# A one-core decoder layer kernel: its opening put in order of need, with small tables loaded later from the pool's queue

## What is computed

```
h = rmsnorm(x); h @ w_in -> [q_B | k_B | v_B | u_A | v_A | q_C | gate logits]
A: chunked gMLP gating, u * (W_s v + b), causal 128x128 W_s per group
B: dilated sliding-window attention with a relative bias; C: cross-attention into 256 memory rows
x = x + w_out( sig(g_A) P_A(A) + sig(g_B) P_B(B) + sig(g_C) P_C(C) )
x = x + MoE(rmsnorm(x))    top-4 of 32 experts;   y = rmsnorm(x)
memory keys and values: rmsnorm(mem_prompt) @ w_mem_kv
```

## Time and profile before

| | |
|---|---|
| median of 3 runs | 1539.71 us (1538.79 to 1542.64) |
| the profiled execution | 1539.54 us, span 1537.7 us |
| PE busy | 1409.7 us (92%) |
| ACT busy | 240.7 us (16%) |
| DVE busy | 374.8 us (24%) |
| POOL busy | 52.6 us (3%) |
| DMA | 515.17 MB, mean 335 GB/s |
| mean granted PE clock | 0.953 |

### The profile page before, as it was taken

One profiled execution on the slowest core, in us unless ns is written; L12 is line 12 of the kernel. 1 busy time (PEld: TensorE's weight loads), 2 busy tenths in 40 slices (PEclk: granted clock), 3 DMA queues, 4 the chain that ended last, 5 costly groups with the idle time before them and its releaser, 6 DMA issues.

```text
span 1537.7 us, 20357 instructions
## 1 busy us (share of the span) xinstructions
PE 1409.7 (92%) x8013; PEld 693.9 (45%) x8013; DVE 374.8 (24%) x858; ACT 240.7 (16%) x389; POOL 52.6 (3%) x90
## 2 busy tenths in 40 slices
PE   3999977997898779999999999999999999999995
PEld 1685535866786334343343433333343333333333
DVE  2100365420012152222222212222221222222123
ACT  2001011220001041121111111111121111112112
POOL 0100212002100000000000000000000000000000
PEclk9999877996599989999999999999999999999998
DMA  9535966239247657999999999999999999999994
GB/s 319 181 128 191 328 236 237 89 157 345 94 163 288 261 207 310 424 422 421 422 422 422 421 423 421 422 422 422 422 422 422 422 422 422 421 422 422 422 422 164
DMA packets 86697, 515.17 MB, mean 335 GB/s; under 512 B 10047, under 2 KB 11655, under 8 KB 36812
## 3 DMA queue, kind: packets, MB, share of 16 engines
q1 hardware_dynamic: 77504, 493.69, 79.3%
q0 software_dynamic: 6016, 18.83, 3.8%
q10 hardware_dynamic: 3148, 2.24, 0.5%
HBM read 511.21 MB, written 47.52 MB: 363 GB/s over the span
## 4 chain that ended last, share of the span: by engine, by line
PE 65%; DMA 21%; DVE 5%; SPq 4%; issue 2%; ACT 1%; ACTq 1%; POOL 0%; DVEq 0%
PE psum L524 62%; DMA weights<-in_w_gate_up 17%; SPq L424 4%; PE psum L527 3%; DMA weights<-in_w_out 2%; DMA weights<-in_cache_mem_kv 2%; DVE qk L1272 1%; ACTq L1325 1%; ACT qk L1328 0%; POOL weights L484 0%; DVE x L1297 0%; DVE kvt L1166 0%; DVE va L1179 0%; DVE hT L1242 0%; DVE kc L1177 0%
## 5 line engine op out<-in xcount | busy, mean ns | idle before, releaser
L524 PE MATMUL psum<-weights,wsp 128*64 128x512 f32 x2048 | 491.8, 603 | 15.2 <-DMA weights<-in_w_gate_up 14.4
L524 PE MATMUL psum<-weights,merged 128*64 128x512 f32 (+2 forms) x1152 | 274.3, 600 | 10.7 <-DMA weights<-in_w_out 9.2
L524 PEld LDWEIGHTS psum<-weights,wsp 128*64 128x64 f32 x2048 | 127.5, 136 | 266.8 <-issue 177.9
L1242 DVE TENSOR_TENSOR hT<-psum,hT 128x264 f32<-128x264 f32 x264 | 101.7, 427 | 529.4 <-PE psum L524 529.3
L524 PE MATMUL psum<-hT,weights 128*128 128x264 f32 x704 | 171.7, 403 | 13.8 <-DVE weights L984 9.1
L524 PEld LDWEIGHTS psum<-weights,merged 128*64 128x64 f32 (+2 forms) x1152 | 89.6, 141 | 167.0 <-issue 158.9
L524 PEld LDWEIGHTS psum<-hT,weights 128*128 128x128 f32 x704 | 138.2, 198 | 45.6 <-DVE weights L984 12.2
L524 PE MATMUL psum<-bT,merged 64*128 64x264 f32 x528 | 94.2, 434 | 1.1 <-ACT merged L1487 0.7
L1468 ACT COPY bT<-psum 128x264 f32<-128x264 f32 x33 | 12.5, 379 | 484.1 <-PE psum L527 484.0
L524 PEld LDWEIGHTS psum<-bT,merged 64*128 64x128 f32 x528 | 39.8, 184 | 106.7 <-issue 103.9
L1272 DVE TENSOR_SCALAR qk<-psum,lowest 128x512 f32<-128x512 f32 x64 | 48.0, 750 | 162.6 <-PE psum L524 159.2
(11 more groups left out here) (242 smaller groups left out, 765.3 us busy)
## 6 DMA issues: line engine op xcount, KB each, us to landing
weights<-in_w_gate_up SPq DMA_DIRECT2D x256, 1024.0 KB, 26.1
weights<-in_w_down SPq DMA_DIRECT2D x128, 1024.0 KB, 25.0
out<-in_cache_win_kv SPq DMA_DIRECT2D x8, 4094.0 KB
weights<-in_w_in SPq DMA_DIRECT2D x13, 2048.0 KB, 7.7
weights<-in_cache_mem_kv POOLq DMA_DIRECT2D x16, 512.0 KB, 7.8
out<-in_cache_win_kv SPq DMA_DIRECT2D x2, 4088.0 KB
weights<-in_cache_win_kv POOLq DMA_DIRECT2D x48, 128.0 KB, 6.1
weights<-in_w_mem_kv SPq DMA_DIRECT2D x2, 2048.0 KB, 14.4
```

Source lines behind the costliest of these rows:

```text
L524: return nc.tensor.matmul(out, lhsT, rhs, start=start, stop=stop, **kw)
L1242: V.tensor_tensor(acc[:, c, :], p_a[j % 2][part], acc[:, c, :], ALU.add).then_inc(s_acc, 1)
```

## The change

The list of steps begins with `vec` and `memT`; a step `xn` (root and scaling of x) stands between `memT` and `kc`; `rel`, `sbias` and `wsp` come between `q` and `k`. The memory rows arrive in two DMAs of 128 rows with a semaphore each. Ten table loads go from ACT's queue to POOL's, behind a wait for x. SP no longer waits for tables behind its first block. ACT runs one Sqrt on an unused column of `stat` before it waits for the memory rows.

```diff
--- before.py
+++ after.py
@@ -111,10 +111,9 @@
 
 def schedule():
 
-    s = [("vec",), ("wsp",)] + [("rel", g) for g in range(NG)] + [("sbias",)]
-    s += [("memT", k) for k in range(KD)] + [("kc", h) for h in range(CH)] + [("xT", k) for k in range(KD)]
+    s = [("vec",)] + [("memT", k) for k in range(KD)] + [("xn",)] + [("kc", h) for h in range(CH)] + [("xT", k) for k in range(KD)]
     s += [("vc", t) for t in range(2)] + [("kct", t) for t in range(2)]
-    s += [("q", m) for m in range(6)] + [("k", m) for m in range(6)]
+    s += [("q", m) for m in range(6)] + [("rel", g) for g in range(NG)] + [("sbias",), ("wsp",)] + [("k", m) for m in range(6)]
     s += [("v", t, 0) for t in range(3)] + [("v", t, 1) for t in range(3)]
     s += [("kt", t, n) for t in range(3) for n in range(2)] + [("qc", m) for m in range(4)]
     s += [("qs", 0), ("qs", 1), ("qcs",), ("vts",), ("selfb",)]
@@ -322,7 +321,8 @@
         s_sq, s_vecr, s_wsp, s_rel, s_sels, s_lnw, s_bsp, s_w00 = (sem("in_" + n) for n in (
             "square", "vectors", "wsp", "rel", "sample", "lnw", "bsp", "w00"))
         s_router_in, s_gfin_in, s_brow_in, s_grow_in = sem("in_router"), sem("in_gfin"), sem("in_brow"), sem("in_g_ffn_row")
-        s_mem_in, s_x_in, s_xagain = sem("in_mem"), sem("in_x"), sem("in_x_again")
+        s_mem_in = [sem(f"in_mem{t}") for t in range(2)]
+        s_x_in, s_xagain = sem("in_x"), sem("in_x_again")
         s_block_in = [sem(f"block_in{n}") for n in range(4)]
         s_chunk_in = [sem(f"chunk_in{n}") for n in range(CHUNKS)]
         s_used = sem("chunks_used")
@@ -363,7 +363,8 @@
         @block.sync
         def _(sp):
             with nc.allow_non_contiguous_dma(reason="small vectors"):
-                sp.dma_start(mem_tok, I["mem_prompt"][0].rearrange("(t p) c -> p t c", p=P)).then_inc(s_mem_in, 16)
+                for t in range(2):
+                    sp.dma_start(mem_tok[:, t, :], I["mem_prompt"][0, t * P:(t + 1) * P, :]).then_inc(s_mem_in[t], 16)
                 sp.dma_start(x1[:, 0:2, :], I["x_prompt"][0].rearrange("(t p) c -> p t c", p=P)).then_inc(s_x_in, 16)
                 sp.dma_start(x1[0:NS, 2, :], I["x_sample"][:, 0, :]).then_inc(s_x_in, 16)
             copies = []
@@ -384,11 +385,6 @@
                 if n >= 4:
                     sp.wait_ge(s_job, last_job[n - 4])
                 sp.dma_start(block_view(name, src.shape[0]), src).then_inc(s_block_in[n % 4], 16)
-                if n == 0:
-                    sp.wait_ge(s_vecr, 48)
-                    sp.wait_ge(s_wsp, 16)
-                    sp.wait_ge(s_rel, 32)
-                    sp.wait_ge(s_sels, 16)
                 if 10 <= n and copies:
                     shift(*copies.pop(0))
                 if name == "gc1":
@@ -467,6 +463,19 @@
         def _(pool):
             nc.gpsimd.iota(iota[:], [[1, SLOTS * PASSES]], base=1, channel_multiplier=0,
                            allow_small_or_imprecise_dtypes=True).then_inc(s_iota, 1)
+            pool.wait_ge(s_x_in, 32)
+            with nc.allow_non_contiguous_dma(reason="small vectors"):
+                pool.dma_start(wsp[:], I["w_spatial"][0].rearrange("g i j -> i g j")).then_inc(s_wsp, 16)
+                pool.dma_start(rel[0:REL_BUCKETS, :], I["rel_bias"]).then_inc(s_rel, 16)
+                pool.dma_start(selh.rearrange("p g x -> p (g x)"), C["hankel"]).then_inc(s_rel, 16)
+                pool.dma_start(sels.rearrange("p g x -> p (g x)"), C["sample"]).then_inc(s_sels, 16)
+                pool.dma_start(lnw[:, 0, :], I["ln_v_g"].to_broadcast([P, 512])).then_inc(s_lnw, 16)
+                pool.dma_start(lnw[:, 1, :], I["ln_v_b"].to_broadcast([P, 512])).then_inc(s_lnw, 16)
+                pool.dma_start(bsp[:].rearrange("p g i -> p (g i)"),
+                              I["b_spatial"].rearrange("d g i -> d (g i)").to_broadcast([P, AG * P])).then_inc(s_bsp, 16)
+                pool.dma_start(w00[:], I["w_spatial"][:, :, 0, 0].to_broadcast([P, AG])).then_inc(s_w00, 16)
+                pool.dma_start(wr[:], I["w_router"][0].rearrange("(k p) e -> p k e", p=P)).then_inc(s_router_in, 16)
+                pool.dma_start(br[:], I["b_router"].to_broadcast([P, E])).then_inc(s_router_in, 16)
             taken(pool, "rel", NG - 1)
             pool.dma_start(rel_rows[:].rearrange("g h x -> h g x"), hrow).then_inc(s_hstore, 16)
             pool.wait_ge(s_hstore, 16)
@@ -902,14 +911,6 @@
                 if t == 0:
                     seq(ins)
             ins.then_inc(s_done["memn"], 1)
-            rms_scale(stat[:, 2:5], D, 5)
-            dve.wait_ge(s_rt, 2)
-            seq(V.reciprocal(stat[:, 2:5], stat[:, 2:5]))
-            for t, (_, tn) in enumerate(TILES):
-                ins = V.tensor_scalar(x1[0:tn, t, :], x1[0:tn, t, :], stat[0:tn, 2 + t:3 + t], None, ALU.mult)
-                if t < 2:
-                    seq(ins)
-            ins.then_inc(s_done["xn"], 1)
 
             for s in steps:
                 kind, a = s[0], s[1:]
@@ -940,6 +941,15 @@
                     k, = a
                     ready()
                     V.tensor_scalar(memT[:, k, :], o[:, 0:NM], g_mem[:, k:k + 1], None, ALU.mult).then_inc(free, 1)
+                elif kind == "xn":
+                    rms_scale(stat[:, 2:5], D, 5)
+                    dve.wait_ge(s_rt, 2)
+                    seq(V.reciprocal(stat[:, 2:5], stat[:, 2:5]))
+                    for t, (_, tn) in enumerate(TILES):
+                        ins = V.tensor_scalar(x1[0:tn, t, :], x1[0:tn, t, :], stat[0:tn, 2 + t:3 + t], None, ALU.mult)
+                        if t < 2:
+                            seq(ins)
+                    ins.then_inc(s_done["xn"], 1)
                 elif kind == "xT":
                     k, = a
                     ready()
@@ -1312,25 +1322,15 @@
                 act.dma_start(sq[:], C["square"]).then_inc(s_sq, 16)
                 for n, name in enumerate(("norm_mix", "norm_mem", "norm_ffn")):
                     act.dma_start(vecr[n * KD:(n + 1) * KD, :], I[name][0].rearrange("(k p) -> k p", p=P)).then_inc(s_vecr, 16)
-                act.dma_start(wsp[:], I["w_spatial"][0].rearrange("g i j -> i g j")).then_inc(s_wsp, 16)
-                act.dma_start(rel[0:REL_BUCKETS, :], I["rel_bias"]).then_inc(s_rel, 16)
-                act.dma_start(selh.rearrange("p g x -> p (g x)"), C["hankel"]).then_inc(s_rel, 16)
-                act.dma_start(sels.rearrange("p g x -> p (g x)"), C["sample"]).then_inc(s_sels, 16)
-                act.dma_start(lnw[:, 0, :], I["ln_v_g"].to_broadcast([P, 512])).then_inc(s_lnw, 16)
-                act.dma_start(lnw[:, 1, :], I["ln_v_b"].to_broadcast([P, 512])).then_inc(s_lnw, 16)
-                act.dma_start(bsp[:].rearrange("p g i -> p (g i)"),
-                              I["b_spatial"].rearrange("d g i -> d (g i)").to_broadcast([P, AG * P])).then_inc(s_bsp, 16)
-                act.dma_start(w00[:], I["w_spatial"][:, :, 0, 0].to_broadcast([P, AG])).then_inc(s_w00, 16)
-                act.dma_start(wr[:], I["w_router"][0].rearrange("(k p) e -> p k e", p=P)).then_inc(s_router_in, 16)
-                act.dma_start(br[:], I["b_router"].to_broadcast([P, E])).then_inc(s_router_in, 16)
 
             def squares(dst, src, junk):
                 A.activation(junk, src, ACT.Square, accum_out=dst).then_inc(s_ss, 1)
 
             junk = merged[:, :, :].rearrange("p a b -> p (a b)")
             act.wait_ge(s_dve, 1)
-            act.wait_ge(s_mem_in, 16)
+            A.activation(stat[:, 39:40], stat[:, 39:40], ACT.Sqrt)
             for t in range(2):
+                act.wait_ge(s_mem_in[t], 16)
                 squares(stat[:, t:t + 1], mem_tok[:, t, :], junk[:, t * D:(t + 1) * D])
             act.wait_ge(s_ms, 1)
             A.activation(stat[:, 0:2], stat[:, 0:2], ACT.Sqrt).then_inc(s_rt, 1)
@@ -1338,8 +1338,6 @@
             junk2 = qk[:, :, :].rearrange("p a b -> p (a b)")
             for t, (_, tn) in enumerate(TILES):
                 squares(stat[0:tn, 2 + t:3 + t], x1[0:tn, t, :], junk2[0:tn, t * D:(t + 1) * D])
-            act.wait_ge(s_ms, 2)
-            A.activation(stat[:, 2:5], stat[:, 2:5], ACT.Sqrt).then_inc(s_rt, 1)
 
             for s in steps:
                 kind, a = s[0], s[1:]
@@ -1351,7 +1349,10 @@
                     def take(out, in_, name, n=n, free=free):
                         act.wait_ge(s_job, n + 1)
                         A.copy(out, in_).then_inc(free, 1)
-                if kind == "rel":
+                if kind == "xn":
+                    act.wait_ge(s_ms, 2)
+                    A.activation(stat[:, 2:5], stat[:, 2:5], ACT.Sqrt).then_inc(s_rt, 1)
+                elif kind == "rel":
                     take(hrow[:, a[0], :], o[0:HPG, 0:HANK], "hrow")
                 elif kind == "kc":
                     take(kcT[:, a[0], :], o[:, 0:NM], "kcT")

```

## The result

| | before | after |
|---|---|---|
| median, first runs | 1539.25 us, 4 runs (1538.56 to 1542.64) | 1524.22 us, 4 runs (1523.43 to 1524.48) |
| ratio | | 0.9895, 95% interval 0.9879 to 0.991 |
| the profiled execution | 1539.54 us, span 1537.7 | 1524.09 us, span 1522.3 |
| PE busy | 1409.7 us | 1407.8 us |
| POOL busy | 52.6 us | 59.5 us |

15.0 us less by the medians, 15.5 by the profiled executions and 16.2 by the ratio (13.9 to 18.6 by its interval), against 17.8 forecast: inside the range.

What follows compares the result with a forecast made beforehand. ACT's queue, issuing DMAs, was taken to bound the opening, PE everything from kc on. 21.5 gained less 3.7 lost gave 17.8 us: 1539.54 - 17.8 = 1521.7, given as 1521.8; range 1517.5 to 1527.5.

Steps and rivals of the forecast that it cites:

- The hinge: Start of kc in the opening: at 15.7 instead of 37.24 us, held by memk's landing, bringing all behind forward; 21.5 gained.
- the tables' share: In memk's landing: POOL's tables share the last 2 us of its transfer, adding 0.6 us.
- The fit of the Trainium skill: memk's transfer as 2.0 us plus bytes at 436 GB/s: landing at 13.1, memT then bounds; as a rival 1520.3, 17%.
- ACT's chain: In the opening: both table loads leave the path, memory rows squared and scaled by 9.85, when memT's part begins.
- The rival of a dummy without effect: In ACT's opening: each table load still stands, 14.3 becomes 16.6, kc one us later, 1522.7; 3%.
- Scaling of x: Behind memT on DVE: done at about 17, covered by kc until 31.5; without that cover it would cost 2.9.
- kc's own time: PE's kc step: its 15.83 us stay, with the same slow start wherever kc starts.
- What comes back: Between q and k: rel, sbias and wsp cost their full length on PE, 3.7 us lost; bounds 3.4 and 7.0.
- The rival of light jobs at half rate: Between q and k: rel, sbias and wsp slow PE, costing 7.0, k's slow start about 2 more; 1527, 10%.
- SP and POOL: DMA queues: SP's earlier issues and POOL's later streams cause no wait, costing nothing.
- The slower rival (tables late): At rel: PE waits for tables past 71.5, slower than before past 89.3; landed at 95 gives 1545; 3%.
- The rest follows 1 to 1: Behind the opening: weight blocks and the last stage move with PE, so the gain converts 1 to 1.

Runs made afterwards that it cites:

- e5: The changed kernel with memk issued on SP's queue in front of the rows of x; 1522.47 us, ratio 0.9875 to the kernel before.
- e10: The changed kernel with POOL's table loads waiting for memk's landing instead of x's; 1523.77 us, ratio 0.9881 to the kernel before.
- e2: The changed kernel without the early Sqrt on an unused column; 1526.84 us, ratio 0.989 to the kernel before.
- e1: The changed kernel run again, unaltered; 1524.36 us, ratio 0.9873 to the kernel before.
- e4: The changed kernel with root and scaling of x put back in front of the copies of vec and memT; 1529.34 us, ratio 0.9906 to the kernel before.
- e8: The kernel before, unaltered, run for a second profile; 1543.74 us, ratio 1.0008.
- e12: The kernel before, unaltered, run for a third profile; 1542.08 us, ratio 0.9994.
- e3: The changed kernel with SP's wait for vectors and tables put back behind its first block; 1524.67 us, ratio 0.988 to the kernel before.
- e7: The changed kernel with the ten tables issued on ACT's queue behind its squares of x, not on POOL's; 1523.12 us, ratio 0.9875 to the kernel before.
- e11: The kernel before with only the ten table loads moved to POOL's queue behind x; 1533.65 us, ratio 0.9933 to the kernel before.
- e6: The changed kernel with PE's old job order (vec, wsp, rel, sbias, then memT); 1532.68 us, ratio 0.994 to the kernel before.
- e9: e5's kernel with rel, sbias and wsp put one by one behind k jobs 0 to 4; 1522.53 us, ratio 0.9876 to the kernel before.

## Why the prediction was right, point by point

**The hinge.** kc's start was given as 15.7, held by memk; it is 15.62, held by memk (15.6 to 16.2 in the five profiles in which memk holds it). e5 shows the cause: with 1.08 MB less in front, PE no longer waits for it. The 0.6 us for the tables' share was wrong in its reason (e10: none), and the 15.1 without it was 0.4 early. The fit of the Trainium skill ("DMA: Bandwidth & Descriptors", anatomy of one DMA), which gave 13.1 and kc at 14.3, was 2.4 us short of the landing; that section gives it for DMAs issued from POOL's queue, and memk is issued from SP's.

**ACT's chain.** memT at 9.85 was 10.24: the second half landed 0.3 later than 6.5. Both table loads are off the path, as said. The rival of a dummy without effect was sized right at its place (16.6 against e2's 16.92) but not behind it: its 1522.7 took no account of the clock. e2 is 2.5 us slower than e1.

**Scaling of x.** Its cover was kc; it is done at 17.6. Without the move it costs 5.0 (e4). I had priced the loss of the cover at 2.9, as if only the scaling stood in front of memT; the wait for x's squares, 13.3 us, stood there too.

**kc's own time.** The prediction kept kc's 15.83 us and expected its slow start everywhere. It is 15.88 in the kernel after, but 13.9 in both later profiles of the kernel before (e8, e12). Against those, kc starts 22.8 us or more earlier in e1 and takes 1.7 longer, so sdiag is still 17.5 to 17.7 earlier. That the sum met sdiag to a tenth is partly the luck of the first pair; against the later profiles it holds to 0.3.

**What comes back.** rel, sbias and wsp were given 3.7 us; k started 21.4 - 17.8 = 3.6 later, relative to q. The rival of light jobs at half rate did not come about in this profile but did in e2 and e5, where rel to sdiag took 1.6 us more. I had given 2 for k's slow start and a further 3.3 for the jobs themselves; the second part did not show, since the clock fell only near the end of the jobs.

**SP and POOL.** Nothing hung on either: e3 within 0.3 us by the medians, and POOL's later streams did not stall sk. The slower rival (tables late) was far off: POOL's ten issues took 0.5 to 1.2 us each. Three of them ran while DVE scaled x. The first of the three (`w`, L476) took 1.19 us, against 0.76 in e10 with no DVE work beside it, and the scaling 2.51, against 2.32 in e7 with no issue of POOL beside it. Of the hold that the Trainium skill describes ("SBUF — State Buffer", the "DVE blocks DMA" trap) this case shows at most these tenths of a microsecond.

**The rest follows 1 to 1.** This is the step with an error: 17.8 us of forecast stood at sdiag to a tenth, and 15.4 of them at the end of the first pair of profiles. Its term should have been 17.8 plus or minus 2 to 3 for the clock's behaviour behind each idle stretch. In the medians of e1 and its kernel before, 18.7 reach the end. What is shown: the pieces where it goes in the first pair (the w_out wait and the half rate behind it), and that the kernel before has the same forms (e12) and scatters by as much. Whether the change makes the longer form more frequent stays open.

## What to carry to other kernels

An engine that has work to do should not stand in its own DMA queue: issue what the first chain needs, and the rest behind that chain's last step, on POOL's queue or its own (e11, e7). Then order each engine's steps by need; here moving the tables alone gave 10 us and the other parts 9 more. When the compute chain is short enough, the next bound is the order of bytes in the weight queue: add up the megabytes in front of the first weights at the rate of the rows, and look at what stands ahead of the first weights (e5 brought kc 1.0 us forward and kept 1.4 at sdiag, too little to show in the time).

## What was not expected of the hardware

- The granted clock reads 1.00 in every window of the opening, yet wsp's transposes take 421 ns there and 273 later. kc, the same 64 instructions, took 15.7 us in the first profile of the kernel before and 13.9 in the other two.
- kc started slow in all five profiles in which PE waited for memk between memT and kc (after, e1, e3, e7, e10: 15.3 to 15.9 us). Where memT ran straight into kc it was at full rate at once in six (e2, e5, e6, e8, e9, e12: 13.9) and slow in three (before, e4, e11: 15.7 to 16.0). The wait for memk may thus have cost more than its length; no run here tests that.
- Behind three rel jobs, with sbias and wsp, all in a row for 3.6 us, the granted clock fell to 0.50 in e2 and e5 and not in after, e1, e3, e4, e7 and e10. It fell where kc had started at full rate.
- The first table load stood behind the wait for the rows (e2: 5.44), and an earlier instruction without that wait hid it. The load for the root did not stand behind its wait: it starts at 8.94 in e2, as the DVE step that the root waits for (8.95) only begins, and in the kernel before it starts at 20.66, with that DVE step at 20.68 (rows below). Which waits hold a load back is not shown.
- The router bias's load holds ACT's queue 8.1 to 9.5 us in the four profiles looked at (before, e7, e8, e12), and POOL's 0.6.

The load for the root in the kernel before, and the DVE step that the root waits for:

```profile
20.66 1.28 ACT L1336 ACT_TABLE_LOAD   x1
20.68 0.17 DVE L890 TENSOR_SCALAR stat<-stat 128x2 f32<-128x2 f32 x1 [19.49 <-ACT merged L1328]
```
